# Retimed steps in the hand-timed delta order: the last head's decays and scan, and the second head's value SiLU

## What is computed

```python
q = l2norm(heads(silu(causal_depthwise_conv(dq, conv_q)), 128))
k = l2norm(heads(silu(causal_depthwise_conv(dk, conv_k)), 128))
v = heads(silu(causal_depthwise_conv(dv, conv_v)), 256)
decay = exp(where(incl, g[..., :, None] - g[..., None, :], -inf))
lower = where(strict, einsum('nbhid,nbhjd->nbhij', k * beta, k) * decay, 0)
sol = triangular_solve(eye + lower, [v * beta, k * beta * exp(g)])
# scan over the chunks, state S of 128 x 256 per head
v_new = u_c - w_c @ S;  o = q_dec @ S + attn @ v_new;  S = S * g_last + k_dec.T @ v_new
o_dn = rmsnorm(o, gain) * silu(heads(dz, 256));  merged += o_dn @ w_branch_dn
```

## Time and profile before

| | us |
|---|---|
| median of the runs (3) | 2828.59 |
| lowest, highest | 2822.67, 2834.78 |
| profiled execution | 2822.94 |
| its span | 2821.1 |
| PE busy in the span | 2745.4 (97%) |
| DVE, ACT, POOL busy | 1485.7, 1144.8, 476.2 |
| DMA, mean rate | 86 GB/s |

### The profile page before, as it was taken

One profiled execution on the slowest core, in us unless ns is written; L12 is line 12 of the kernel. 1 busy time (PEld: TensorE's weight loads), 2 busy tenths in 40 slices (PEclk: granted clock), 3 DMA queues, 4 the chain that ended last, 5 costly groups with the idle time before them and its releaser, 6 DMA issues.

```text
span 2821.1 us, 37389 instructions
## 1 busy us (share of the span) xinstructions
PE 2745.4 (97%) x14613; PEld 2225.4 (79%) x14613; DVE 1485.7 (53%) x2101; ACT 1144.8 (41%) x1709; POOL 476.2 (17%) x281
## 2 busy tenths in 40 slices
PE   8999999999999999998999999999999999999999
PEld 4888888876667788887888888888878877788887
DVE  6734535256667533337655566653267765644443
ACT  4221212225564422234655555554366663432221
POOL 0000000011002000003434454433422222100000
PEclk9999999999999999999999999999999999999999
DMA  6422313234113332323211121111211113233232
GB/s 237 149 83 77 123 63 105 65 114 144 46 38 143 97 97 88 100 90 105 66 53 48 51 68 61 61 46 38 83 54 59 60 54 107 90 99 96 91 101 77
DMA packets 69872, 241.79 MB, mean 86 GB/s; under 512 B 8218, under 2 KB 8346, under 8 KB 69314
## 3 DMA queue, kind: packets, MB, share of 16 engines
q1 hardware_dynamic: 62032, 221.28, 24.4%
q10 hardware_dynamic: 7666, 18.13, 1.9%
HBM read 232.74 MB, written 6.64 MB: 85 GB/s over the span
## 4 chain that ended last, share of the span: by engine, by line
PE 85%; DVE 7%; ACT 6%; issue 1%; DMA 1%; ACTq 0%; DVEq 0%; POOL 0%; SPq 0%; POOLq 0%
PE ps L1113 62%; PE ps L1511 3%; PE ps L1612 2%; PE ps L1408 2%; PE ps L1448 2%; PE ps L1315 1%; PE ps L1336 1%; PE ps L1440 1%; PE ps L1143 1%; ACT r L466 1%; DVE UT L473 1%; ACT w_hi L466 1%; DVE f_t L484 1%; PE ps L1469 1%; ACT DT L466 1%
## 5 line engine op out<-in xcount | busy, mean ns | idle before, releaser
L1113 PE MATMUL ps<-Nh,w_hi 128*128 128x512 f32 (+1 forms) x1808 | 660.0, 365 | 9.3 <-DVE Nl L473 4.9
L1113 PE MATMUL ps<-Nl,w_hi 128*128 128x512 f32 (+1 forms) x1808 | 629.6, 348 | 0.0
L1113 PE MATMUL ps<-Nh,w_lo 128*128 128x512 f32 (+1 forms) x1808 | 627.5, 347 | 0.0
L466 ACT ACTIVATE w_hi<-w_raw 128x1024 fp32r<-128x1024 f32 (+1 forms) x352 | 368.2, 1046 | 638.4 <-PE ps L1113 522.4
L473 DVE TENSOR_TENSOR w_lo<-w_raw,w_hi 128x1024 fp32r<-128x1024 f32 (+1 forms) x242 | 299.3, 1237 | 281.1 <-ACT w_hi L466 271.1
L1113 PEld LDWEIGHTS ps<-Nh,w_hi 128*128 128x128 f32 x1808 | 342.2, 189 | 80.1 <-issue 29.9
L1113 PEld LDWEIGHTS ps<-Nl,w_hi 128*128 128x128 f32 x1808 | 342.1, 189 | 50.5 <-issue 5.8
L1113 PEld LDWEIGHTS ps<-Nh,w_lo 128*128 128x128 f32 x1808 | 342.0, 189 | 44.2
L473 POOL TENSOR_TENSOR w_lo<-w_raw,w_hi 128x1024 fp32r<-128x1024 f32 x110 | 270.9, 2463 | 604.0 <-ACT w_hi L466 600.2
L1113 PE MATMUL ps<-x1h,w_hi 128*128 128x512 f32 (+1 forms) x784 | 272.1, 347 | 2.3 <-DVE x1l L484 2.3
L1113 PE MATMUL ps<-x1l,w_hi 128*128 128x512 f32 (+1 forms) x784 | 266.5, 340 | 0.0
(11 more groups left out here) (358 smaller groups left out, 4660.5 us busy)
## 6 DMA issues: line engine op xcount, KB each, us to landing
w_raw<-in_w_in SPq DMA_DIRECT2D x132, 512.0 KB, 3.5
w_raw<-in_w_proj SPq DMA_DIRECT2D x89, 512.0 KB, 3.5
w_raw<-in_w_ada SPq DMA_DIRECT2D x52, 512.0 KB, 4.0
w_raw<-in_w_out SPq DMA_DIRECT2D x48, 448.0 KB, 3.2
w_raw<-in_w_out SPq DMA_DIRECT2D x24, 512.0 KB, 3.5
w_raw<-in_w_mix_in SPq DMA_DIRECT2D x19, 512.0 KB, 3.5
w_raw<-in_w_bdn SPq DMA_DIRECT2D x16, 512.0 KB, 3.5
w_raw<-in_w_mix_out SPq DMA_DIRECT2D x8, 512.0 KB, 3.5
```

Source lines behind the costliest of these rows:

```text
L466: self.then_inc(self.e.activation(out, in_, func, **kw), sem)
L1113: ins = e.matmul(out[:, 512 * j:512 * j + n], a[:, kk, :], x[:, kk, c0:c0 + n], start=k == 0 and p == 0, stop=k == nt - 1 and p == 2)
```

## The change

It edits only tables of times and two expressions that choose them. For head 7 the two decay events come earlier, with a table of their own. The table of the last but one group (group 6: preparation of head 7 and scan of head 6) gets later and more even times. The SiLU of head 2's values (`siluv` with i = 0) leaves the end of group 0 and stands in group 1 behind three products.

```diff
@@ -65,6 +65,7 @@
 DECAYS = ((66, "bcast"), (73, "decay"))
+LAST_DECAYS = ((62, "bcast"), (69.65, "decay"))
@@ -78,18 +79,17 @@
 L2_FIRST = ((21.01, "siluz"), (22.55, "siluqk"), (25.3, "l2q"), (25.3, "lnq"), (27.1, "stq0"), (30.4, "stq1"),
-            (30.4, "stq2"), (37, "l2k"), (40, "lnk"), (45.3, "stk0"), (45.9, "stk1"), (45.9, "stk2"),
-            (59.1, "siluv"))
+            (30.4, "stq2"), (37, "l2k"), (40, "lnk"), (45.3, "stk0"), (45.9, "stk1"), (45.9, "stk2"))
-LATE_PREPARE = ((1.35, "pair"), (6.9, "turn"), (9.6, "x1"), (11.2, "u1"), (17.7, "x2"), (22.2, "u2"),
-                (28.2, "x3"), (32.7, "u3"), (35.7, "x4"), (40.2, "u4"), (46.7, "x5"), (49.7, "u5"),
-                (56.9, "x6"), (60.5, "u6"))
-LATE_SCAN = ((7.95, "v0"), (7.95, "siluv"), (7.95, "s0"), (7.95, "k1"), (9.83, "v1"), (12.1, "s1"),
-             (16.67, "k2"), (19.21, "v2"), (23.63, "s2"), (27.41, "k3"), (28.59, "v3"), (31.72, "s3"),
-             (32.73, "k4"), (39.25, "v4"), (44.52, "s4"), (45.66, "nsq"), (48.43, "norm"), (58.57, "gain0"),
-             (59.51, "gain1"), (59.51, "parts"), (63.7, "hiz"))
+LATE_PREPARE = ((1.35, "pair"), (8.5, "turn"), (11, "x1"), (14.3, "u1"), (21, "x2"), (26.5, "u2"),
+                (33, "x3"), (38, "u3"), (42, "x4"), (46.5, "u4"), (51, "x5"), (55, "u5"),
+                (59.5, "x6"), (64, "u6"))
+LATE_SCAN = ((3, "v0"), (3.1, "siluv"), (5.5, "s0"), (9.5, "k1"), (13, "v1"), (17, "s1"),
+             (23, "k2"), (25, "v2"), (30, "s2"), (32, "k3"), (36, "v3"), (40, "s3"),
+             (42, "k4"), (45, "v4"), (49, "s4"), (50, "nsq"), (53, "norm"), (61, "gain0"),
+             (62, "gain1"), (62, "parts"), (66, "hiz"))
@@ -189,9 +189,9 @@
-        after = []
+        after = [(3, "siluv", 0)] if i == 1 else []
         if i + 2 < NH:
-            steps += [(at, s, i + 2) for at, s in DECAYS]
+            steps += [(at, s, i + 2) for at, s in (DECAYS if i + 3 < NH else LAST_DECAYS)]
```

## The result

The changed kernel takes 2832.36 us (median of 12 runs, 2828.13 to 2835.34), the kernel before 2826.12 us, also in 12 runs. The ratio is 1.0021 with a 95% interval of 1.0013 to 1.0028: 6 us slower. I had forecast 2.4 us faster. That is a miss in sign, inside the 0.5% named as the bound. Against the kernel before I was off by 8.6 us, against the time itself by 6.2: the first three runs had put the median of before at 2828.59, 2.5 us higher.

A forecast was written before the change was run, and what follows sets the result against it. PE, busy for 97% of the span, was taken as the bound; 0.9 us from part 1 and 1.5 us from parts 2 and 3 made 2.4 us won from a median of 2828.59: 2826.2 us, range 2815.5 to 2834.

The forecast's parts named there:

- The two places with the large waits: PE's waits for `V` in group 1, 4.41 us, and for `UT` at the start of group 6, 3.5 us.
- The pause at unit 41: PE stands 3.2 us at unit 41, formerly 0.1, because ACT's `vv` queues behind head 7's decays.
- The decays' start: Head 7's decays on ACT can start at 1890.6, 4.1 us after the second DMA issue, 3.5 us sooner.
- The table load that runs while ACT waits: Group 6, before head 7's `x1`: the load adds nothing; by the skill page `x1` would come up to 2.7 us later.
- DVE's chain from the mask to `AT`: Group 6: DVE's `pair` starts about 1900.0 and ends 1905.8; `AT` of the four chunks frees its bank about 1903.8.
- part 2: Head 7's decays earlier: `pair` on DVE starts about 1900.0 instead of 1900.50, half a microsecond won.
- Parts 2 and 3: Head 7's earlier decays and group 6's even times: together 1.5 us won, bounds -2.5 and +5.
- The ceiling: The most to win at the two places in groups 1 and 6: 16 us, 0.57% of the time.
- Part 1: Group 1, SiLU of head 2's values behind three products: 0.9 us won, range 0 to 1.65.
- (c): Half clock from unit 41 until about 1906 makes it slower: 2 to 4 us lost, 2831; chance 0.20.
- (d): Nothing moves because DVE's `pair` binds the order in both groups: 2828.6, within 1 us; chance 0.10.
- (b): `vv` at unit 41 is not held, PE meets only short pauses: wins 8 to 14 us, 2817; chance 0.18.

The follow-up runs named there:

- e5: Changed kernel with three POOL steps at the turn from group 5 to 6 cut short, output incomplete; ratio to before 1.0001.
- e9: Changed kernel with POOL's remainders put behind the first level of head 7, which waits for `AT`; ratio to before 0.9997.
- e10: Kernel before with head 7's decays early and POOL's remainders deferred for heads 2 to 7, first level waiting for both `AT`; 2814.82 us, ratio 0.9961.
- e11: e10 plus the change's move of the SiLU of head 2's values; 2810.89 us, ratio to before 0.9950.
- e2: Kernel before with only the two decay events of head 7 moved as in the change; ratio to before 0.9996.
- e12: e9 with group 6's even table mended around `k3`, `x6` and the first `v` of head 7; ratio to before 0.9993.
- e4: Kernel before with head 7's decay DMAs issued some 10 us earlier and the decays run ahead of unit 46's copies; ratio to before 1.0004.

## Why the prediction was wrong, step by step

**What held.** The two places with the large waits. The pause at unit 41: 3.2 us forecast, 3.28 measured, released by `vv`. The decays' start, 4.1 us after the second issue (1890.46 to 1894.54). The table load that runs while ACT waits. In group 1, 1.9 us for `V` and then two pieces for `AT`: 1.96, 1.02 and 0.75. At `k3` 0.6 forecast, 0.63 measured; at `x6` about 1.5, and 1.57. The last row belongs to a term that I had left out:

```profile
1940.28 0.70 PE L1457 MATMUL ps<-S,qk 128*128 128x256 f32 x2 [0.63 <-DVE S L484]
1969.13 1.13 PE L1408 MATMUL ps<-UT,LM 128*128 128x128 f32 x8 [1.57 <-issue]
1979.87 0.70 PE L1469 MATMUL ps<-vb,UT 128*128 128x256 f32 x2 [1.09 <-DVE UT L473]
```

**The term that failed: DVE's chain from the mask to `AT`, in part 2.** I wrote that `pair` on DVE would start at 1900.0 and end at 1905.8, and took for every step the length that its row in the trace of before shows. In the new trace it starts at 1906.10; less the 3.9 us by which the new trace lies behind at that point, that is 1902.2. `AT` of the four chunks ends at 1911.21, so 1907.3 against my 1903.8: 3.5 us late. The L2 step (+0.96), the taps (+1.17) and the subtraction (+1.08 over its 1.63 of before) are 3.2 of them. The pause at `s0` was so 3.65 instead of 1.9 us, and `x1` came at 1918.31 - 3.9 = 1914.4 instead of 1910.2. What POOL would be doing beside DVE's steps at their new times does not enter that part of the prediction at all; POOL is looked at only for `ol`. A length taken from a row where an engine happened to be idle, or waited for something else, was the price of that row and not of the step. e5 and e9 show that this term carries the loss: with DVE's steps short again, 6 us of it are gone.

**Terms left out.** The first `v` of head 7 waits 1.09 us for `u6`'s step on DVE, which I had not priced. Again POOL: `gain1` takes 2.93 us and `parts` 3.43 beside two remainders of 5.18 us in all. The first branch of head 6 waits 0.30 us for `ol`, of the 0 to 2.5 given. Parts 2 and 3 were forecast at 1.5 us won and lost 5.1. Of these 6.6 us, 4.2 are the late `x1` and 1.4 the two waits just named; about 1 us behind `x1` I cannot place. The ceiling left out the four waits of 1.2 us for `AT` in groups 2 to 5, which e10 took away.

**Part 1** was forecast at 0.9 us, and gave -0.2 by the traces. The pauses were right; the half clock behind them lasted 6.8 us, and the result lies just past the bad end of my range (0).

**The rivals.** (c), slower, named the point from which it decides: `x1` later than 1912.6. It was 1914.4, and the kernel is slower, by more than its 2 to 4 us. But its mechanism, half clock from the pause at unit 41 to about 1906, did not come: the clock was at half from 1899.9 to 1903.3 and again from 1910.1, which is 1896.0 to 1899.4 and from 1906.2 in the times of before. (c) has `x1` late through the clock; the runs show it late through DVE's chain. (d) was right that DVE's `pair` sets the time in both groups, and wrong that nothing would move. (b) fell. The measured median of 2832.36 lies in the range given, which was made wide enough for (b) and (c) both; that says nothing for the forecast.

## What to carry to other kernels

When a step is moved to fill an engine's idle time, look at what the neighbour that shares its memory port did in that time: the idle microseconds may be where the neighbour's work was free. Take a step's length from rows with the same neighbour running, and give both ends, alone and beside it. Before retiming a chain on DVE, try to move POOL's work that is not urgent out of it: in this kernel that alone gave 6 us, and two edits that were worth nothing by themselves gave 3 to 4 us each on top of it.

## What the runs showed of the hardware

- A DVE step with both inputs in SBUF that begins while POOL is at work ends just behind POOL's step. The one on 16 rows and 16 columns took 1.04 to 1.13 us so, and 0.16 us while POOL was idle (1490.43 in e11) or just between two steps (1911.53 in the changed kernel). A step with an input in PSUM kept its 0.69 us in either case. The waiting counts as DVE's busy time. That the step waits for the POOL instruction to end fits all 80 steps counted above; that it is the port and not something else in common was not shown apart from the rule cited.
- The granted clock fell to 1.2 GHz, mostly for 3.4 us and twice for 6.8, in stretches where PE was busy throughout (1794 and 1879 in the changed kernel, 1624 and 1710 in e2, none in before). From 1380 to 2060 the 14 profiles have 20 of them, and each began 2.9 to 4.3 us behind a pause of 0.21 us for `vv` at the start of a second value unit. There are five such pauses in each profile, so 50 of the 70 had nothing behind them. A spell of 3.4 us costs 1.7 us. One profile against another is thus good to a few microseconds in its span, and to tenths in a single pause.
- Like pauses were followed by unlike spells of half clock. With the pause of 3.0 to 3.3 us at unit 41 it lasted 3.4 us in the changed kernel, e5, e9 and e12, and 6.8 us in e2. With 4.4 us for `V` in group 1 it lasted 3.4 us in before and four other runs, and 6.8 us in e2 and e4. What sets the length was not settled.
